# Where squares are summed, which value buffer a page takes, and when keys are turned, in a decoder step on one core

## What is computed

```python
def _rmsnorm(x, w):
    return x * lax.rsqrt(jnp.mean(x * x, axis=-1, keepdims=True) + NORM_EPS) * w

def _decoder_layer(x, c, pos, ret_s0, moba_mix, ...):
    sh1, sc1, g1, sh2, sc2, g2 = split(silu(c) @ w_mod + b_mod, 6)      # w_mod 1024 x 6144
    h = _rmsnorm(x, norm1_w) * (1 + sc1) + sh1
    rq, rk, rv, rg, mq, mk, mv = split(h @ w_in)                        # w_in 1024 x 3584
    ret_out, ret_s = _retention_branch(rq, rk, rv, rg, pos, ret_s0, ret_gn_w)
    moba_out = _rmsnorm(moba_mix(mq, mk, mv), moba_norm_w)              # by head
    x = x + g1 * (concat([ret_out, moba_out]) @ w_out)
    h2 = _rmsnorm(x, norm2_w) * (1 + sc2) + sh2
    x = x + g2 * ((silu(h2 @ w_gate) * (h2 @ w_up)) @ w_down)           # d_ff 2816
    return x, mk, mv, ret_s
# y = _rmsnorm(x, final_w), for the prompt and for the samples
```

## Time and profile before

| | us |
|---|---|
| runs | 1035.85, 1039.37, 1046.96 |
| median | 1039.37 |
| profiled execution, time | 1034.07 |
| its span | 1032.2 |
| mean granted clock of TensorE | 0.976 |
| busy: PE, DVE, ACT, POOL | 961.6, 624.5, 338.4, 139.4 |

### The profile page before, as it was taken

How to read it: one execution, slowest core, us unless ns; L and a number is a source line. 1 busy time by engine, 2 the same in 40 slices (tenths; PEclk the granted TensorE clock), 3 DMA queues, 4 the chain that set the end, 5 groups by cost and what they waited for, 6 DMA issues and landing times.

```text
span 1032.2 us, 20974 instructions
## 1 busy us (share of the span) xinstructions
PE 961.6 (93%) x7919; PEld 675.8 (65%) x7919; DVE 624.5 (60%) x1067; ACT 338.4 (33%) x735; POOL 139.4 (14%) x129
## 2 busy tenths in 40 slices
PE   3879998999999987979989999999999999999996
PEld 2557775766666644547756767676777777777775
DVE  1566874677767667876788584432655555453244
ACT  5412233334333624542252152332333222121113
POOL 0011111444210132204151220000000000000000
PEclk9899999999999989999989899999999999999998
DMA  9978877999786889988998668778476988787652
GB/s 340 364 257 282 284 252 268 296 274 300 255 287 215 276 320 390 356 288 280 362 320 285 231 230 265 230 228 267 144 218 167 240 226 231 218 251 248 204 194 87
DMA packets 217973, 269.14 MB, mean 261 GB/s; under 512 B 13473, under 2 KB 168425, under 8 KB 209682
## 3 DMA queue, kind: packets, MB, share of 16 engines
q1 hardware_dynamic: 110226, 126.65, 38.7%
q10 hardware_dynamic: 98432, 74.04, 23.6%
q0 software_dynamic: 9216, 67.11, 17.7%
HBM read 260.04 MB, written 5.64 MB: 257 GB/s over the span
## 4 chain that ended last, share of the span: by engine, by line
PE 72%; DVE 8%; DMA 7%; issue 5%; SPq 4%; DVEq 2%; ACT 1%; POOLq 1%; POOL 1%; ACTq 0%
PE banks L1128 13%; PE banks L1129 12%; PE banks L1130 12%; PE banks L1078 6%; PE banks L1216 4%; PE banks L1141 4%; PE banks L1143 4%; PE banks L1142 4%; PE banks L1161 4%; DVE KT L1846 3%; DMA V<-in_cache_v 3%; DMA K<-in_cache_k,kidx 1%; SPq L420 1%; PE banks L1340 1%; DMA early<-in_w_mod 1%
## 5 line engine op out<-in xcount | busy, mean ns | idle before, releaser
L658 ACT ACTIVATE whi<-raw 128x1024 fp32r<-128x1024 f32 (+1 forms) x76 | 78.6, 1035 | 298.0 <-PE banks L1130 144.4
L1128 PE MATMUL banks<-ahi,whi 128*128 128x512 f32 x416 | 169.2, 407 | 0.1
L1846 DVE STREAM_TRANSPOSE KT<-K 128x2048 f32<-128x2048 f32 x63 | 145.5, 2310 | 30.0 <-DMA K<-in_cache_k,kidx 15.1
L1129 PE MATMUL banks<-alo,whi 128*128 128x512 f32 x416 | 163.5, 393 | 0.0
L1130 PE MATMUL banks<-ahi,rawlo 128*128 128x512 f32 x416 | 163.3, 393 | 0.0
L1809 DVE TENSOR_TENSOR rawlo<-raw,whi 128x1024 fp32r<-128x1024 f32 (+1 forms) x76 | 91.3, 1201 | 54.3 <-ACT whi L658 51.2
L523 POOL DMA_INDIRECT K<-in_cache_k,kidx x64 | 64.0, 1000 | 412.4 <-DVE KT L1846 363.7
L1128 PEld LDWEIGHTS banks<-ahi,whi 128*128 128x128 f32 x416 | 78.7, 189 | 31.2 <-issue 13.1
L1141 PE MATMUL banks<-ahi,whi 128*128 128x512 f32 x216 | 90.2, 417 | 1.2 <-DVE rawlo L1816 0.9
L1130 PEld LDWEIGHTS banks<-ahi,rawlo 128*128 128x128 f32 x416 | 78.8, 189 | 17.3
L1161 PE MATMUL banks<-KT,qbd 128*32 128x128 f32 x2048 | 74.0, 283 | 15.7 <-DVE KT L1846 13.0
(11 more groups left out here) (330 smaller groups left out, 1462.1 us busy)
## 6 DMA issues: line engine op xcount, KB each, us to landing
V<-in_cache_v SPq DMA_DIRECT2D x184, 256.0 KB
rawm<-in_w_mod ACTq DMA_DIRECT2D x14, 1024.0 KB
raw<-in_w_in ACTq DMA_DIRECT2D x12, 1024.0 KB
zT<-in_cache_v SPq DMA_DIRECT2D x48, 256.0 KB
raw<-in_w_gate ACTq DMA_DIRECT2D x22, 512.0 KB
raw<-in_w_up ACTq DMA_DIRECT2D x22, 512.0 KB
srw<-in_w_gate SPq DMA_DIRECT2D x22, 512.0 KB, 5.6
srw<-in_w_up SPq DMA_DIRECT2D x22, 512.0 KB, 7.3
```

What stands on the lines that cost most here:

```text
L658: act.activation(whi[t % 2][:, 0:kd, :], raw[u][:, 0:kd, t % 2 * P:(t % 2 + 1) * P], ACT.Copy).then_inc(s_hi, 1)
L1128: pe.matmul(out[:, :], whi[t % 2][:, k, :], hi(k), start=(first and n == 0), stop=False)
L1129: pe.matmul(out[:, :], whi[t % 2][:, k, :], lo(k), start=False, stop=False)
L1846: dve.transpose(KTb[:, :, :, :], Kb[g % 2][:, :]).then_inc(s_kt, 1)
```

## The change

Eight edits.

1. Sample page rows `kidx` are computed by DVE behind the first four `act_lo`, and two blocks of the first norm's output (k = 5, 7) are staged by DVE instead of ACT.
2. `keep_mod` is one copy of 128x256; the quarters are added by `turn_mod`, which multiplies with a matrix of ones (`sum_pv`) in place of transposing.
3. In the first slots keys(1) stand ahead of mod_chunk(2) on PE, keys(2) behind the first half of tile 2, and on DVE the modulation's steps ahead of turn_keys(3).
4. A third ring for values for groups 17 to 27 (`LANE`).
5. In retention one turn of keys goes ahead of the block selection (group 34), and group 43 is turned ahead of the last pair's splitting.
6. Norm behind the out-projection: POOL adds the squares of blocks 0 to 6 up in `rb`, one addition and a drain for each block right behind a gather; PE sums only `rb` and the last block.
7. Group 60's keys are turned earlier in slot 59.
8. Last norm by feature: behind each down tile DVE multiplies x2T with final_w into `x3w`, ACT squares x2T, POOL adds the squares; 18 of the 32 transposes stand between down tiles 21 and 22, one sum, one root for all positions, and the scaling of four stores' data is shared by ACT and DVE.

```diff
+RING_2 = {g: (1, 5)[(g - 17) % 3] for g in range(17, 28) if (g - 17) % 3 < 2}
+RING_2.update({g: 2 if g < 32 else 3 if g < 53 else 4 for g in range(29, NG, 2)})
+LANE = lambda g: 0 if g not in RING_2 else 2 if RING_2[g] == 5 else 1
...
-            if g == 27:
+            if g == 18:
                 sp.wait_ge(s_md, NMOD)
...
+        def add_squares(k):
+            pool.wait_ge(s_sqx, k + 1)
+            pool.tensor_tensor(rb[:, :], rb[:, :], stage[k % 2][:, :], ALU.add)
+            pool.drain().then_inc(s_sqa, 1)
...
+        def add_x3_squares(k):
+            pool.wait_ge(s_sqx, X3Q + k + 1)
+            pool.tensor_tensor(x3q(0), x3q(0), x3q(k), ALU.add)
+            pool.drain().then_inc(s_sqa, 1)
...
+            if 1 <= g - R_OUT - 4 < KT - 1:
+                add_squares(g - R_OUT - 4)
...
-                if f >= 3:
-                    act.wait_ge(s_ssm, f - 2)
-                act.activation(stage[(f - 1) % 2][:, :], x2T[:, f - 1, :], ACT.Square).then_inc(s_sqx, 1)
+                if f >= 4:
+                    act.wait_ge(s_sqa, f - 3)
+                act.activation(rb[:, :] if f == 1 else stage[(f - 1) % 2][:, :], x2T[:, f - 1, :], ACT.Square).then_inc(s_sqx, 1)
...
+        x3_squares(KT - 1)
+        act.wait_ge(s_r1, X3I + 1)
+        act.activation(st2[:, 24:28], st2[:, 16:20], ACT.Sqrt).then_inc(s_r2, 1)
+        act.drain()
+        for i in (0, 2):
+            act.wait_ge(s_yt, 1)
+            act.activation(ytok[i][:, :].rearrange("p (e c) -> p e c", e=2), TURNED[i][:, :, :], ACT.Copy,
+                           scale=st2[:, 24 + i:25 + i]).then_inc(s_yr, 1)
...
-                last = pe.transpose(out[:, 32 * f:32 * f + 32], mst[0:32, f * P:(f + 1) * P], ident[0:32, 0:32])
+                last = pe.matmul(out[:, 32 * f:32 * f + 32], mst[:, f * P:(f + 1) * P], C("sum_pv"), start=True, stop=True)
...
+        def sum_squares():
+
+            pe.matmul(DB[:, 0:TT], ident, C("pad0")[:, 0:TT], start=True, stop=False, skip_group_check=True)
+            pe.wait_ge(s_sqa, KT - 2)
+            sum_over_features(DB, rb, False)
+            pe.wait_ge(s_sqx, KT)
+            sum_over_features(DB, stage[1], True).then_inc(s_ssm, 1)
...
-            fold_groups(mst[0:32, CHUNK * (n % 2):CHUNK * (n % 2 + 1)], src, s_mev)
+            then(cp(mst[:, CHUNK * (n % 2):CHUNK * (n % 2 + 1)], src[:, 0:CHUNK])).then_inc(s_mev, 1)
...
+            if hp == 1:
+                slot_head(s)
...
                 slot_head(s + 2)
+                slot_head(R_HEADS)
+                slot_rest(R_HEADS)
+                split_out(0)
                 act_lo(0, KT + 4)
                 act_lo(1, KT + 5)
                 dve.drain()
-                split_out(0)
-            slot_head(s + 3)
...
-        slot_rest(R_HEADS)
+            if hp in (1, 2):
+                slot_head(s + 3)
...
+            ts(x3w(k)[:, :], x2T[:, k, :], vT[:, V_FW + k:V_FW + k + 1], None, ALU.mult).then_inc(s_nx, 1)
...
+        dve.wait_ge(s_ssm, X3S + 1)
+        then(ts(st2[:, 16:20], TURNED[TT - 1][:, 1, 0:TT], 1.0 / DM, EPS, ALU.mult, ALU.add))
+        dve.reciprocal(st2[:, 16:20], st2[:, 16:20]).then_inc(s_r1, 1)
```

More of the change, by code:

```diff
@@ L342, in decoder_step @@
     s_k = [sem(f"k_loaded{i}") for i in range(2)]
-    s_v = [sem(f"v_loaded{i}") for i in range(8)]
+    s_v = [sem(f"v_loaded{i}") for i in range(12)]
     s_kt, s_lg, s_own, s_s1 = sem("k_turned"), sem("logits"), sem("own_logits"), sem("block_sums")
@@ L384, in values @@
     def values(g):
-        if g in RING_2:
-            return rings[RING_2[g]], s_v[4:8], sum(x <= g for x in RING_2)
-        return rings[0], s_v[0:4], g + 1 - sum(x <= g for x in RING_2)
+        n = LANE(g)
+        return rings[RING_2.get(g, 0)], s_v[4 * n:4 * n + 4], sum(LANE(x) == n for x in range(g + 1))
     def values_before(g):
-        return max((x for x in range(g) if (x in RING_2) == (g in RING_2)), default=None)
+        return max((x for x in range(g) if LANE(x) == LANE(g)), default=None)
     def w_buffer(c):
@@ L615, in _ @@
                 masked_k(b + 1)
+        for k in range(1, KT - 1):
+            add_x3_squares(k)
     @block.scalar
@@ L1054, in _ @@
             sample_slot(R_DOWN + d)
-        for i in range(TT):
-            act.wait_ge(s_yt, i + 1)
-            act.activation(ytok[i][:, :].rearrange("p (e c) -> p e c", e=2), TURNED[i][:, :, :], ACT.Square, accum_out=st[:, 16 + i:17 + i])
-            act.drain()
-            act.activation(st2[:, 16 + i:17 + i], st[:, 16 + i:17 + i], ACT.Sqrt, scale=1.0 / DM, bias=C("eps")).then_inc(s_yr, 1)
+            fb, e = divmod(d - 5, 6)
+            if fb >= 0 and e < 2:
+                x3_squares(2 * fb + e)
+        x3_squares(KT - 1)
[6 more added lines that the diff above has]
+                           scale=st2[:, 24 + i:25 + i]).then_inc(s_yr, 1)
     @block.tensor
@@ L1714, in _ @@
             sample_slot(R_DOWN + d)
-        for i in range(TT):
-            for k in range(KT):
-                if i == 0 and k == 0:
-                    pe.wait_ge(s_ev, F_DOWN + 7 + 2)
-                if i == 0 and k == KT - 1:
-                    pe.wait_ge(s_ev, F_DOWN + 8 + 2)
-                last = pe.transpose(TURNED[i][:, k // 4, (k % 4) * P:(k % 4 + 1) * P], x2T[:, k, i * P:(i + 1) * P], ident)
-            last.then_inc(s_yt, 1)
+            if d == 6 * DM // CHUNK - 3:
+                pe.wait_ge(s_x3, 1)
+                pe.wait_ge(s_nx, X3W + KT - 2)
+                for i in range(TT - 1):
+                    for k in range(KT - 2):
+                        turn_x3(i, k)
+        pe.wait_ge(s_nx, X3W + KT - 1)
+        for i in range(TT - 1):
+            turn_x3(i, KT - 2)
+        for k in range(4):
+            turn_x3(TT - 1, k)
+        pe.wait_ge(s_nx, X3W + KT)
+        for i in range(TT - 1):
+            last = turn_x3(i, KT - 1)
+        last.then_inc(s_yt, 1)
+        sums = TURNED[TT - 1][:, 1, :]
+        pe.matmul(sums[:, 0:TT], ident, C("pad0")[:, 0:TT], start=True, stop=False, skip_group_check=True)
+        pe.wait_ge(s_sqa, X3A + KT - 2)
+        sum_over_features(sums, x3q(0), False)
+        pe.wait_ge(s_sqx, X3Q + KT)
+        sum_over_features(sums, x3q(KT - 1), True).then_inc(s_ssm, 1)
+        pe.wait_ge(s_r1, X3I + 1)
+        for k in range(4, KT):
+            last = turn_x3(TT - 1, k)
+        last.then_inc(s_yt, 1)
     @block.vector
@@ L1791, in _ @@
         gains(0, 4, 8, V_N1)
-        dve.wait_ge(s_pt, 16)
-        dve.wait_ge(s_ident, 16)
-        for g in range(GRP):
-            q = slice(32 * g, 32 * g + 32)
-            last = ts(kidx[q, :], pt[q, :].rearrange("p (n g) -> p n g", g=GRP)[:, :, g], 32.0, C("row32")[q, :], ALU.mult, ALU.add)
-        last.then_inc(s_idx, 1)
         def act_lo(k, n):
@@ L1963, in _ @@
             act_lo(k, k)
+        dve.wait_ge(s_pt, 16)
+        dve.wait_ge(s_ident, 16)
+        for g in range(GRP):
+            q = slice(32 * g, 32 * g + 32)
+            last = ts(kidx[q, :], pt[q, :].rearrange("p (n g) -> p n g", g=GRP)[:, :, g], 32.0, C("row32")[q, :], ALU.mult, ALU.add)
+        last.then_inc(s_idx, 1)
         early_modulation(1)
@@ L2363, in evict_down @@
             residual(2 * fb + half, 40 + 2 * fb + half, bank[2 * (fb % 2) + half])
+            k = 2 * fb + half
+            dve.drain()
+            ts(x3w(k)[:, :], x2T[:, k, :], vT[:, V_FW + k:V_FW + k + 1], None, ALU.mult).then_inc(s_nx, 1)
         for d in range(6 * DM // CHUNK):
```

80 lines of the change are left out of this document (48 added, 32 removed).

## The result

The changed kernel took 1056.55 us (median of four runs, 1054.29 to 1059.83), the kernel before 1041.23 in the runs beside it: a ratio of 1.0155, with a 95% interval of 1.0113 to 1.0198. That is 16 us longer, above the range of 1030 to 1053. The forecast's direction was right (slower), its size was a quarter of what came.

What follows compares the result with a forecast made beforehand. TensorE was taken as the bound, busy 961.6 of 1032.2 us. Start -4, modulation +3, retention -5, out-projection norm +7.5 and tail +2.4 sum to +3.9, giving 1043 us on a median of 1039.4, range 1030 to 1053.

Steps and rivals of the forecast that it cites:

- a chain of six links: Norm behind the out-projection: six additions each wait out their gather's landing (7 us), hand-overs 1.0 us together; +7.5 us.
- one wait: Start: TensorE's 1.59 us wait for the modulation copy goes, part of -4 us forecast there.
- the other: Retention: TensorE's 2.20 us wait for a key turn behind the block selection, counted within -5 us forecast there.
- the one row: Out-projection: the gather issued at 489.52 let VectorE's turn begin 6.9 us later, read as its landing time.

## What to carry to other kernels

Before a drain or a barrier goes on an engine that also issues transfers, ask what is in flight there: here each one cost what was left of a 1 MB gather, and with a semaphore on the instruction itself, waited for by the next one, nothing was left that could be told from zero. When a term is a chain of six links, price the whole link, with the hand-over at its end and the clock behind the wait: here half a microsecond in each landing and half a microsecond in each hand-over made 6 us. And where a wait is removed or a step is moved ahead, look up when the other transfers of that place land: here a chunk of weights took over one wait, and a gather made the other longer.

## What was not expected of the hardware

A GpSimd operation that posts its own semaphore is not held by a gather ahead of it on the same list: posted and used by TensorE 2.3 us after the gather's issue, while with a drain in its place TensorE could begin only 7.3 us after it, 0.1 us behind the landing. The gathers' landing grew no shorter when only one was outstanding: 5.7 to 8.8 us, 7.5 in the mean, at a transfer share of 0.72 and 0.55, where the one row had 6.9 us at 0.91.
